# Starting each tile's front six steps early in the period before, spreading its selection over more steps, and loading the sample's inputs in another order

## The reference, cut to what matters

```
sc = einsum('thcd,hcnd->thcn', qry, keys); sv, si = top_k(sc, 16)      # 8 heads, 2 halves, 128 keys
cand = sv[:, :, 0, :, None] + sv[:, :, 1, None, :]                     # 16 x 16 sums per head
fv, fi = top_k(cand.reshape(..., 256), 16); eidx = take(cidx, fi); gate = softmax(fv)
ue, ve = u[eidx], v[eidx]                                              # 8 * 16 = 128 experts per token
act = gelu(einsum('thkd,td->thk', ue, xb))
y = einsum('thk,thkd->td', gate * act, ve)                             # rows of 1024 floats
```

## Time and profile before

| what | value |
|---|---|
| median of 3 runs | 3381.01 us (3380.08 to 3386.39) |
| profiled execution | 3388.74 us, span 3386.9 us |
| busy in the span | PE 87%, DVE 62%, POOL 61%, ACT 45% |
| HBM traffic | 361 GB/s over the span |
| mean granted PE clock | 0.959 |

### The profile page before, as it was taken

How to read it: one execution, slowest core, us unless ns; L and a number is a source line. 1 busy time by engine, 2 the same in 40 slices (tenths; PEclk the granted TensorE clock), 3 DMA queues, 4 the chain that set the end, 5 groups by cost and what they waited for, 6 DMA issues and landing times.

```text
span 3386.9 us, 31486 instructions
## 1 busy us (share of the span) xinstructions
PE 2953.4 (87%) x8213; PEld 1396.8 (41%) x8213; DVE 2104.8 (62%) x4852; ACT 1528.1 (45%) x4155; POOL 2073.1 (61%) x2162
## 2 busy tenths in 40 slices
PE   8888999889997899889997898789978997589976
PEld 6754444334443454335443443334433442244221
DVE  2345555856566566856685657766776668364594
ACT  2313653357423663357334753465336633252333
POOL 2003666666656666666667766776677667464675
PEclk9889999999999999999998999999989998798999
DMA  8307999999999999999999999999999999899998
GB/s 313 137 15 270 398 375 361 343 408 405 394 329 388 410 399 372 359 410 405 399 341 389 409 410 396 369 409 409 400 360 410 409 408 356 313 366 340 356 349 349
DMA packets 358876, 1222.63 MB, mean 361 GB/s; under 512 B 42747, under 2 KB 65244, under 8 KB 357404
## 3 DMA queue, kind: packets, MB, share of 16 engines
q0 software_dynamic: 308288, 1121.46, 85.5%
q1 hardware_dynamic: 22540, 66.55, 5.2%
q10 hardware_dynamic: 27872, 32.61, 2.9%
HBM read 1195.69 MB, written 25.79 MB: 361 GB/s over the span
## 4 chain that ended last, share of the span: by engine, by line
PE 47%; DMA 18%; DVE 15%; POOL 7%; issue 7%; ACT 5%; SPq 0%; ACTq 0%; DVEq 0%; POOLq 0%
PE ps L1091 24%; DMA rows<-in_peer_v,idx 11%; PE ps L973 7%; DMA rows<-in_peer_u,idx 5%; PE ps L857 5%; DVE rows L1497 5%; PE ps L956 4%; POOL rows L469 4%; POOL rows L479 3%; PE ps L810 2%; DVE r L1343 1%; DVE r L1338 1%; DVE r L1378 1%; PE ps L833 1%; DVE r L1379 1%
## 5 line engine op out<-in xcount | busy, mean ns | idle before, releaser
L1091 PE MATMUL ps<-rows,diag 128*128 128x512 f32 (+1 forms) x4224 | 2042.5, 620 | 329.8 <-DMA rows<-in_peer_v,idx 152.3
L1497 DVE CUSTOM_DVE_ANT_0 rows<-rows,ps 128x1024 f32<-128x1024 f32 x1056 | 1261.2, 1216 | 638.4 <-DMA rows<-in_peer_u,idx 635.6
L479 POOL DMA_INDIRECT rows<-in_peer_v,idx x1056 | 1028.5, 974 | 602.1 <-PE ps L1091 384.5
L469 POOL DMA_INDIRECT rows<-in_peer_u,idx x1056 | 1019.4, 965 | 603.4 <-issue 258.2
L1091 PEld LDWEIGHTS ps<-rows,diag 128*128 128x128 f32 (+1 forms) x4224 | 779.9, 194 | 1437.2 <-issue 1117.0
L747 ACT ACTIVATE act_g<-act_g 128x1 f32<-128x1 f32 x1056 | 211.0, 200 | 1069.6 <-DVE act_g L1497 1052.2
L753 ACT ACTIVATE diag<-ident,act_g 128x128 f32<-128x128 f32 x1024 | 411.2, 402 | 403.4 <-PE ps L1091 377.4
L749 ACT ACTIVATE act_g<-act_g,gate 128x1 f32<-128x1 f32 x1056 | 311.0, 294 | 34.3
L973 PE MATMUL ps<-w_sc,r 128*128 128x512 f32 (+1 forms) x576 | 282.8, 600 | 1.2 <-ACT r L663 1.2
L857 PE MATMUL ps<-rows 128*128 128x416 f32 (+1 forms) x704 | 242.2, 499 | 0.0
L857 PEld LDWEIGHTS ps<-rows 128*128 128x128 f32 x704 | 133.5, 191 | 106.1 <-issue 65.4
(11 more groups left out here) (269 smaller groups left out, 1836.3 us busy)
## 6 DMA issues: line engine op xcount, KB each, us to landing
rows<-in_w_in ACTq DMA_DIRECT2D x42, 512.0 KB, 6.5
rows<-in_peer_u,idx POOLq DMA_INDIRECT x1056, 8.7
rows<-in_peer_v,idx POOLq DMA_INDIRECT x1056, 8.6
r<-proj SPq DMA_DIRECT2D x7, 1344.0 KB, 10.9
proj<-staged ACTq DMA_DIRECT2D x44, 192.0 KB, 5.7
w_sc<-in_w_q_t SPq DMA_DIRECT2D x8, 1024.0 KB, 8.1
rows<-in_w_in POOLq DMA_DIRECT2D x14, 512.0 KB, 5.7
w_o<-in_w_in POOLq DMA_DIRECT2D x10, 512.0 KB, 7.4
```

Of the source, the lines that this page charges most:

```text
L469: nc.gpsimd.indirect_dma_start(ring[:, slot, :], None, a["peer_u"], bass.IndirectOffsetOnAxis(ap=idx[g % 2][:, k:k + 1], axis=0), engine_s ...
L479: nc.gpsimd.indirect_dma_start(ring[:, slot, :], None, a["peer_v"], bass.IndirectOffsetOnAxis(ap=idx[g % 2][:, k:k + 1], axis=0), engine_s ...
L1091: last = nc.tensor.matmul(Y[j][0:m, :], diag[:, n % DIAGS, 0:m], ring[:, slot, 512 * j:512 * (j + 1)], start=(k == 0), stop=(k == steps_of ...
L1497: V.tensor_tensor_reduce(ring[:, slot, :], ring[:, slot, :], hn_u, 1.0, 0.0, ALU.mult, ALU.add, col).then_inc(S["dots"], 1)
```

## The change

Six things are done together.

1. `AHEAD = 6`. The front of every tile starts six steps before the period in which it used to start, so its steps 0 to 5 lie at `k` = 122 to 127 of the period before, and all later ones six steps earlier than they did. Period -1 (front of tile 0, no gathers) gets six more steps at its beginning.
2. The selection is spread: pairs of heads at `q = 118 + 3j`, places at 129, and each of the two groups of three wide operations over three steps (130 to 132, 133 to 135), with the end at 137, the exponential at 132.
3. The blocks move. Tiles 1 and 2 move by six steps. In period 0 seven of twelve blocks, where it was five, stand at steps 23 to 41, and none stands after 104. In period 3 the last four stand at 80, 88, 96, 104, where they were at 88, 99, 110, 121.
4. SP loads projection and keys before it waits for anything else, and stores the finished tile after these loads.
5. For the sample, projection, mask and one-hot table are loaded directly after `topk_done`. The keys follow when ACT has copied tile 7's keys (`k7_kept`, front step 5). The caches are loaded in the period before.
6. The two copies from DRAM to DRAM are issued ahead of the first period.

```diff
+AHEAD = 6
-            0: [29, 33, 37, 41, 45, 86, 92, 98, 104, 110, 116, 122],
+            0: [23, 26, 29, 32, 35, 38, 41, 80, 86, 92, 98, 104],
-            3: [31, 37, 43, 88, 99, 110, 121]}
-FOLD_AT = [5 + 4 * c for c in range(2 * PH)]
+            3: [25, 31, 37, 80, 88, 96, 104]}
+FOLD_AT = [4 * c - 1 for c in range(2 * PH)]
+def front_at(p, k):
+    step, tile = (k + AHEAD) % PICKS, p + 1 + (k + AHEAD) // PICKS
+    return (step, tile) if tile <= TILES else None
...
             def load_sample(f):
+                sp.dma_start(spj, proj_s[:, 0:CHUNKS - 1, :]).then_inc(S["proj_in"], 16)
+                sp.dma_start(s_mask, a["s_mask"]).then_inc(S["caches_in"], 16)
+                sp.dma_start(s_oh, a["s_onehot"]).then_inc(S["caches_in"], 16)
...
+            def load_sample_k(f):
                 sp.wait_ge(S["k7_kept"], 1)
+                sp.dma_start(k_t[:, 1, 0:NS], proj_s[:, CHUNKS - 1, :]).then_inc(S["proj_in"], 16)
...
                 if f is not None:
                     load_front(f)
-                    finish(w)
                     if is_sample(f):
                         load_sample(f)
+                        load_sample_k(f)
+                    finish(w)
...
-                if q == 129:
+                if q == 132:
                     act.wait_ge(S["gate_d"], f + 1)
...
-                    if f is not None:
-                        front(k, f)
+                    if front_at(p, k):
+                        front(*front_at(p, k))
...
-                    if q == 118 + 2 * j:
+                    if q == 118 + 3 * j:
-                if q == 126:
+                if q == 129:
-                    if q == 128 + 2 * j:
+                    if q == 130 + 3 * j:
                         mark(V.tensor_tensor(oh, ..., ALU.is_equal))
+                    if q == 131 + 3 * j:
                         mark(V.tensor_tensor(oh4, oh4, ..., ALU.mult))
+                    if q == 132 + 3 * j:
                         mark(V.tensor_reduce(pos[j][0:n], oh, AX.X, ALU.add))
-                if q == 133:
+                if q == 137:
```

More of the change, by code:

```diff
@@ L72 @@
 LATER = 2 * CHUNKS
-BLOCK_AT = {-1: [96 + 2 * b for b in range(10)],
[4 rows of a table removed]
-FOLD_AT = [5 + 4 * c for c in range(2 * PH)]
+AHEAD = 6
+BLOCK_AT = {-1: [90 + 2 * b for b in range(10)],
[4 rows of a table added]
+FOLD_AT = [4 * c - 1 for c in range(2 * PH)]
 SKEW = 3 * P
@@ L111, in block_at, with steps, time_of @@
     return blocks_before(p, 0) + BLOCK_AT[p].index(k)
+def steps(p):
+    return range(-AHEAD if p < 0 else 0, PICKS)
+def front_at(p, k):
+    step, tile = (k + AHEAD) % PICKS, p + 1 + (k + AHEAD) // PICKS
+    return (step, tile) if tile <= TILES else None
+def time_of(step, f):
+    return (f - 1, step - AHEAD) if step >= AHEAD or f == 0 else (f - 2, step - AHEAD + PICKS)
 def blocks_before(p, k):
@@ L289, in build @@
         s_bias = hn[:, 0:264].rearrange("p (g j) -> p g j", g=KV)
-        s_oh = hn[:, 264:396]
+        s_oh = r3[:, 0:132]
         s_tab = hn[:, 396:652]
@@ L378, in load_front, with load_caches @@
                         sp.dma_start(pj, proj[f, :, 0:CHUNKS - 1, :]).then_inc(S["proj_in"], 16)
+                        sp.wait_ge(S["kv_shifted"], f + 1)
+                        sp.dma_start(k_t[:, 1, :], proj[f, :, CHUNKS - 1, :]).then_inc(S["proj_in"], 16)
+                    if f == 2:
+                        sp.wait_ge(S["block"], CHUNKS)
+                        sp.wait_ge(S["parked"], 16)
+                        sp.dma_start(xn_3, xn_dram).then_inc(S["xn_in"], 16)
+                    if f:
                         sp.wait_ge(S["hn_taken"], f)
                     sp.dma_start(hn[:, :], a["norm_ffn"]).then_inc(S["w_ffn_in"], 16)
-                    if f:
-                        sp.wait_ge(S["kv_shifted"], f + 1)
-                        sp.dma_start(k_t[:, 1, :], proj[f, :, CHUNKS - 1, :]).then_inc(S["proj_in"], 16)
             def load_sample(f):
+                sp.dma_start(spj, proj_s[:, 0:CHUNKS - 1, :]).then_inc(S["proj_in"], 16)
+                sp.dma_start(s_mask, a["s_mask"]).then_inc(S["caches_in"], 16)
+                sp.dma_start(s_oh, a["s_onehot"]).then_inc(S["caches_in"], 16)
                 sp.dma_start(a["v_win_prompt"], v_n[:, 1, :]).then_inc(S["out_kv"], 16)
                 sp.dma_start(a["state_prompt"], state[:, :, :]).then_inc(S["out_kv"], 16)
+            def load_sample_k(f):
                 sp.wait_ge(S["k7_kept"], 1)
+                sp.dma_start(k_t[:, 1, 0:NS], proj_s[:, CHUNKS - 1, :]).then_inc(S["proj_in"], 16)
                 sp.dma_start(a["k_win_prompt"], r3[:, 896:1024]).then_inc(S["out_kv"], 16)
-                for out_name, in_name in (("k_win_sample", "cache_k"), ("v_win_sample", "cache_v")):
-                    sp.dma_start(a[out_name][:, 0:WINDOW - DEC_T, :], a[in_name][:, DEC_T:WINDOW, :])\
-                      .then_inc(S["out_kv"], 16)
+            def load_caches():
                 sp.dma_start(kc_t.rearrange("p (b j) -> p b j", b=DEC_B), a["cache_k_t"].rearrange("b p j -> p b j"))\
@@ L426, in sample_caches @@
                     sp.wait_ge(S[f"st_out{b % 3}"], 16 * (b // 3 + 1))
+            for out_name, in_name in (("k_win_sample", "cache_k"), ("v_win_sample", "cache_v")):
+                sp.dma_start(a[out_name][:, 0:WINDOW - DEC_T, :], a[in_name][:, DEC_T:WINDOW, :])\
+                  .then_inc(S["cache_out"], 16)
             for p in periods:
@@ L440, in _ @@
                     sp.wait_ge(S["h_ready"], f + 1)
+                    if f == TILES - 1:
+                        load_caches()
                     h_at = h_dram[SEQ:TOK, :] if is_sample(f) else h_tiles[f]
@@ L454, in _ @@
             sp.wait_ge(S["y_out"], 16 * (TILES + 1))
-            sp.wait_ge(S["out_kv"], 16 * (3 + 2 + 2 * DEC_B))
+            sp.wait_ge(S["out_kv"], 16 * (3 + 2 * DEC_B))
+            sp.wait_ge(S["cache_out"], 32)
         @block.gpsimd
@@ L757, in _ @@
                 w, g, f = parts(p)
-                for k in range(PICKS):
+                for k in steps(p):
                     if g is not None and k < steps_of(g):
@@ L1096, in _ @@
                 w, g, f = parts(p)
-                for k in range(PICKS + SUM_LAG):
+                for k in [*steps(p), *range(PICKS, PICKS + SUM_LAG)]:
                     if g is not None and 0 <= k - SUM_LAG < steps_of(g):
                         add_row(g, k - SUM_LAG)
-                    if f is not None and k < PICKS:
-                        front(k, f)
+                    if k < PICKS and front_at(p, k):
+                        front(*front_at(p, k))
                     if p == -1 and k in FOLD_AT:
@@ L1389, in sample_front @@
                 q_s, k_s = slots(C_QH, 4, spj).rearrange(flat), slots(C_F, 4, spj).rearrange(flat)
-                if k == 2:
+                if k == AHEAD:
                     for g in range(KV):
@@ L1400, in sample_front @@
                         dve.wait_ge(S["caches_in"], 64)
+                        dve.wait_ge(S["y_ready"], f - 1)
                         if kv:
```

22 lines of the change are left out of this document (7 added, 15 removed), and 4 rows, old and new, of the table BLOCK_AT.

## The result

The changed kernel takes 3362.9 us (3358.13 to 3370.53) where the kernel before, on the same chip, takes 3383.7. It is faster by 0.55%, some 19 us, where 53 us were forecast. The time lies in the range, near its upper end. The sign is right and the size is little more than a third of the forecast.

What follows compares the result with a forecast made beforehand. DMA engines stand short, mostly in the selection, where DVE was taken to hold up the gathers. Terms -45.4 + 5.1 + 12 - 22 - 2.4 = -52.7 us, from the median 3381.0, gave 3328 us; range 3302 to 3364.

Steps and rivals of the forecast that it cites:

- the spread: Selection beside eight tiles: spreading cuts DVE's excess from 18.0 to 12.3 us, winning 5.7 us a tile, 45.4 us in all.
- the early start: Period ends: PE's wait for the keys' load stays hidden with 2.5 us to spare; cost 0, bounds -1 to +1 us a tile.
- the later exponential: Before tile 0's first gather: the exponential stands behind the ninth kept block, so gathers start later; +5.1 us, bounds 0 and 8.
- The sample: Tile 7's stretch: the 29.9 us wait goes, a new wait of 8 us comes; net -22 us, bounds 0 and -30.
- the blocks: Periods 0 and 3: moved blocks load stretches where PE is busy; +9 and +3, together +12 us, bounds 0 and 17.
- DRAM copies: Two copies of 496 KB leave the gathers' time for the nearly idle start; -2.4 us.
- The third rival: Sample's stall changes its place only: the wait at `k` = 126 costs what the load did; 3350 us, chance 0.13.
- may give back up to 5 us: At the first sums: the tenth block's store ahead of the gathers may return up to 5 us; the term kept +5.1.
- The first rival: Selection: POOL's held issues set the loss, not DVE, so the spread gives 0; 3374 us, chance 0.13.
- is busy 49.6 of 70 us only: Selection stretch of tile 5: POOL's busy time, cited as evidence against POOL's held issues setting the loss.
- over 10 us a tile: Sign of error: the prediction is wrong if POOL's issues beside L1338 and L1343 cost more than 10 us a tile.
- The second rival: Tiles 0 to 3, with four or five `u` slots: the spread is worth twice as much there; 3305 us, chance 0.15.

Runs made afterwards that it cites:

- loads_2: The kernel before with only the reordered loads (no early start, no spread, blocks as before), against the kernel before: 0.9929, 3362.4 us.
- early_and_loads: The kernel before with only early start and reordered loads, blocks of before moved six steps earlier with the fronts, against the kernel before: 0.9978, 3376.1 us.
- spread_undone_2: The changed kernel with the selection, exponential included, back on its old steps, against the kernel before: 1.0006, 3388.2 us.
- after_2: The changed kernel unaltered, run again on a chip with the faster memory, against the kernel before: 0.9928, 3360.5 us.
- after_psum_2: The changed kernel with one input of each two-input wide operation moved to PSUM, against the kernel before: 0.9843, 3331.9 us.
- after_psum_blocks: The changed kernel with PSUM inputs, blocks of before moved six steps earlier and exponential at 130, against the kernel before: 0.9815, 3321.5 us.
- no_early_psum_2: The kernel before with reordered loads, spread selection, PSUM inputs and exponential at 130, no early start, old blocks, against the kernel before: 0.9786, 3315.2 us.
- after: The changed kernel as first measured, against the kernel before on the same chip: 0.9945, 3362.9 us; its profiled execution took 3370.53 us.

## Why the prediction was right and wrong

Three terms failed: the spread, counted at -45.4, the early start, counted at 0, and the later exponential, counted at +5.1. The sample and the blocks held. The interval of a measured term, from those of its two ratios, is some 5 to 7 us either way.

| term | forecast | measured | from |
|---|---|---|---|
| sample's loads, DRAM copies | -22 - 2.4 | -24 (0.71%) | loads_2 |
| early start | 0 | +17 (0.49%) | early_and_loads against loads_2 |
| blocks | +12 | +9 (0.28%) | spread_undone_2 against early_and_loads |
| spread with the later exponential | -45.4 + 5.1 | -26 (0.78%); by the traces -5 of it are the exponential's | after_2 against spread_undone_2 |
| sum | -52.7 | -24 | after_2: 0.72% |

**The sample, right.** The loads alone give all that the whole change gives. The new wait is 8.1 us where 8 were forecast. The gain needs neither of the other parts: without the early start L1012 waits 8.8 us. No run has the DRAM copies apart, so their 2.4 us are not shown by themselves. The third rival, a stall that only moves, is out. Tile 7 stayed at 394 us, not 388, as the spread gave it 1.2 us only.

**The exponential, right in the event and wrong in the cost.** The first gather came 5.1 us later, counted from PE's first block, but that cost nothing. `after_2` makes its first dot 5.7 us after `spread_undone_2`. At dot 8 it is 3.7 us ahead, and from dot 16 to dot 88, before the spread changes anything, 4.6 to 5.3 us. `after_psum_2` against `after_psum_blocks` (exponential at 130) shows the same, 6.7 us ahead at dot 16. The step that failed is that moving a store ahead of the gathers "may give back up to 5 us": with the ninth block's store ahead of them it gave back about 10. So the term was -5 us here and not +5.1, outside its bounds. This was seen with the early start only; whether the late exponential pays without it was not run on the faster memory.

**The blocks, right within 3 us.** The charge for two more blocks in a full stretch and one in the scores' steps was in the bounds. Between `early_and_loads` and `spread_undone_2` the loss opens where the blocks stand: -1.1 us at dot 16 of tile 0, 12.3 at dot 56, 8.0 at the end of the tile.

**The spread, the failed step.** The step was "so 5.7 us are won a tile if DVE is what the gathers wait for". Its first half was nearly exact: in tile 5, the 23 steps from dot 91 to dot 114 take 70.8 us where the DMA pace is 58.9, an excess of 11.9 where 12.3 was forecast. The condition did not hold. With less excess on DVE, POOL's four held issues set the loss of 6.7 us. The stretch's loss fell from 12.3 to 70 x (1 - 359/411) = 8.9 us, and tiles 4 to 6 won 3.1 us each between `spread_undone_2` and `after_2`. With the exponential's 5 us taken off, the spread brought some 21 of 45.4 us. The first rival was half right, and its "0" was wrong too. It and the forecast were not alternatives: the two bounds lie over each other in the same stretch, and each hides the other. With both removed the pair is worth 1.0006 to 0.9843, 1.6% or 55 us, more than the 45.4 that I gave to the spread by itself. The evidence I held against the rival misled me: "is busy 49.6 of 70 us only". Between issues POOL shows 0.30 us of idle time that ends with "issue", so a pair takes 2 x (0.94 + 0.30) = 2.48 us against 2.56 us of the DMA pace. By this estimate POOL can win back 0.08 us a step, and a held issue is in effect never made up within the stretch. For the same reason the bound "over 10 us a tile" was set too high, since 7.0 were enough.

The rule of the Trainium skill in the section "Who interferes with whom" of "SBUF — State Buffer", as quoted ahead, speaks for the mechanism. The runs agree: one input in PSUM, and the 2 to 3 us issues become 0.94. That spacing saves nothing is right for the held issues (5.9 us before, 7.0 after), and wrong for the whole, since part of DVE's excess was saved.

**The early start, the second failed step.** I checked the keys' landing at the boundary of tiles 5 and 6, where it is hidden as forecast (in the changed kernel L909 waits at no boundary but the first), and gave 0 to all boundaries. At the first one the gathers have only begun, ACT's shift of the keys stands behind the tenth block, and sums 0 to 2 are not ahead of step 4. The profiled executions of `early_and_loads` and `loads_2` are 22.2 us apart in span, more than the 17, since that of `early_and_loads` was the slowest of its twelve, 11 us above their median. Tiles 0 and 1 account for 15.0 - 8.4 = 6.6 us of it. The rest is spread over tile 2 (3.7 us), tile 3 (5.9 us), tile 7 (6.1 us) and small amounts elsewhere, and the runs don't settle its cause. That the lines of one front now meet other phases of the ring was argued and not shown. With spread and PSUM inputs the early start costs 0.29%, 10 us (`after_psum_blocks` against `no_early_psum_2`), and on the first chip 0.19%, with overlapping intervals; the three sizes agree within their noise. The four terms in the table are steps along one path, and another order would share them out differently.

**The small rings.** The second rival fell: by the spread tiles 1 to 3 gained 2.7, -1.2 and 4.5 us, no more than tiles 4 to 6. Tile 0 shows 12.1 us, but 5.7 of them are its later first dot and 4.9 the exponential's; 1.5 are left.

**The range.** The "own range, from its bounds" of 3312 to 3346 is not what the bounds give. Added up they reach from 3251 to 3404 us, without the early start's 1 us a tile. That the time fell into the wider range of 3302 to 3364 is partly luck: the spread brought some 24 us less and the early start cost 17 us more, while the exponential gave back 10 us where at most 5 were thought of.

## What to carry to other kernels

Where two engines are slow in the same stretch, price the removal of each with the other left in, and of both. Here the PSUM inputs were worth 0 or 0.9% by whether the spread was in. An engine whose idle time ends with "issue" is working, so add that time before calling it free. When a step moves across a boundary, look at each boundary, above all the first, for what then stands ahead of it in the list.

## What the runs showed of the hardware

A DVE operation of 2.29 us with two SBUF inputs stretched an indirect DMA's issue on POOL from 0.94 to as much as 3.04 us (`after`). One of its inputs in PSUM, the first in L1364 and the second in L1370, ended this at the same DVE time (`after_psum_2`). Beside a one-input reduction of 2.28 us (L1373) the issue stayed at 0.94. Two chips ran the same kernel before in 3384 us and two others in 3539 and 3541, and the gain of the loads alone was 0.71% on one of the fast and 0.42% on one of the slow.
